# Hybrid attention step on one core: attention a step further behind the threshold search, index products spread over the heads, gate projection at a step's end, tanh gates

## What is computed

```python
scores = sum_h w_idx[h] * relu(q_idx[h] . k_idx)         # 8 index heads
_, sel = lax.top_k(where(pos_k <= pos_q, scores, -inf), 256)
att  = softmax(q . k[sel] / 8) @ v[sel]                   # 8 query heads, 2 K/V heads
conv = b_conv * conv3(c_conv * u)
mo   = softmax(q_mem . mk / 8) @ mv                       # 4 heads, 256 memory tokens
o = concat[att * silu(g_att), conv * silu(g_conv), mo * silu(g_mem)] @ w_out
y = x + rms_norm(o, g_post)
```

## Time and profile before

| | us |
|---|---|
| median of 3 runs | 2611.46 (2609.06 to 2613.33) |
| profiled execution, its own time | 2617.17 |
| span of the profiled execution | 2615.4 |
| stage A, to about | 690 |
| first output projection starts | 774.4 |
| last output projection starts | 2334.3 |
| TensorE busy, with the modelled ends of matmuls | 2233.5 |
| VectorE busy | 1492.2 |
| ScalarE busy | 1161.4 |
| mean granted TensorE clock | 0.85 |

### The profile page before, as it was taken

One profiled execution on the slowest core, in us unless ns is written; L12 is line 12 of the kernel. 1 busy time (PEld: TensorE's weight loads), 2 busy tenths in 40 slices (PEclk: granted clock), 3 DMA queues, 4 the chain that ended last, 5 costly groups with the idle time before them and its releaser, 6 DMA issues.

```text
span 2615.4 us, 34415 instructions
## 1 busy us (share of the span) xinstructions
PE 2233.5 (85%) x12592; PEld 1762.7 (67%) x12592; DVE 1492.2 (57%) x3449; ACT 1161.4 (44%) x2297; POOL 135.5 (5%) x174
## 2 busy tenths in 40 slices
PE   7999999999478888888988878888878888988765
PEld 4777777776466666676676666666666767768652
DVE  2444444443145666776787777878777842434580
ACT  1111111011025566665776766767577668432000
POOL 0000000000000000000000000000000010100004
PEclk9999999999567788777898989888889889987556
DMA  7111111111511110111011010101010010114001
GB/s 264 66 72 50 70 65 71 47 66 40 180 49 59 53 57 20 50 57 45 17 57 32 28 50 11 49 11 49 11 33 27 17 43 9 43 65 138 1 3 31
DMA packets 58411, 137.57 MB, mean 53 GB/s; under 512 B 13904, under 2 KB 26872, under 8 KB 57248
## 3 DMA queue, kind: packets, MB, share of 16 engines
q1 hardware_dynamic: 56096, 125.26, 14.3%
q0 software_dynamic: 2176, 10.49, 1.2%
HBM read 96.83 MB, written 38.90 MB: 52 GB/s over the span
## 4 chain that ended last, share of the span: by engine, by line
PE 62%; DVE 15%; ACT 13%; issue 6%; DMA 2%; SPq 1%; POOL 1%; PEld 1%; DVEq 0%; ACTq 0%; POOLq 0%; PEldq 0%
PE psum L566 12%; PE psum L599 9%; PE psum L1220 8%; PE psum L1189 7%; PE psum L1231 6%; PE psum L1212 5%; ACT sb_lowj L851 4%; PE psum L1178 3%; PE psum L1202 3%; DVE sb_junk L968 3%; ACT sb_ptb L838 2%; DVE sb_sc L953 2%; ACT sb_p L909 1%; PE psum L613 1%; DVE sb_p L987 1%
## 5 line engine op out<-in xcount | busy, mean ns | idle before, releaser
L1220 PE MATMUL psum<-sb_v,sb_ptb 128*128 128x64 f32 x2176 | 329.9, 300 | 31.0 <-ACT sb_ptb L838 30.6
L1220 PEld LDWEIGHTS psum<-sb_v,sb_ptb 128*128 128x128 f32 x2176 | 315.2, 221 | 49.4 <-ACT sb_ptb L838 48.9
L566 PE MATMUL psum<-sb_w,sb_xt 128*128 128x512 f32 (+5 forms) x1088 | 324.8, 459 | 0.5 <-DVE sb_xt L382 0.5
L851 ACT ACTIVATE sb_lowj<-sb_sc,sb_ncand,sb_scl 128x384 bf16<-128x384 f32 (+13 forms) x224 | 312.5, 1395 | 2.4
L968 DVE TENSOR_SCALAR_CACHE_REDUCE sb_junk<-sb_sc,sb_c 128x384 bf16<-128x384 f32 (+13 forms) x210 | 310.1, 1477 | 3.6
L1212 PE MATMUL psum<-sb_con,sb_p 128*128 128x128 f32 x1280 | 243.6, 320 | 52.6 <-ACT sb_p L909 31.3
L838 ACT ACTIVATE sb_ptb<-psum 128x512 f32<-128x512 f32 (+3 forms) x352 | 187.2, 533 | 185.0 <-PE psum L1212 183.8
L566 PEld LDWEIGHTS psum<-sb_w,sb_xt 128*128 128x128 f32 (+1 forms) x1088 | 178.5, 185 | 134.5 <-issue 125.1
L1231 PE MATMUL psum<-sb_wo,sb_mix 128*128 128x512 f32 x512 | 257.2, 666 | 13.5 <-DVEq L1146 13.5
L1189 PEld LDWEIGHTS psum<-sb_qa,sb_w 128*128 128x128 f32 x2048 | 250.7, 196 | 12.8 <-issue 4.8
L1189 PE MATMUL psum<-sb_qa,sb_w 128*128 128x128 f32 x2048 | 253.0, 280 | 1.3
(11 more groups left out here) (340 smaller groups left out, 2491.4 us busy)
## 6 DMA issues: line engine op xcount, KB each, us to landing
qt_s<-sb_qt SPq DMA_DIRECT2D x32, 512.0 KB, 2.8
sb_x<-in_x_prompt SPq DMA_DIRECT2D x16, 512.0 KB, 3.7
xt_s<-sb_xt SPq DMA_DIRECT2D x16, 512.0 KB, 2.6
sb_qa<-xt_s SPq DMA_DIRECT2D x16, 512.0 KB, 3.3
sb_qa<-qt_s SPq DMA_DIRECT2D x16, 512.0 KB, 3.5
sb_qa<-qt_s SPq DMA_DIRECT2D x32, 256.0 KB, 4.7
sb_xres<-in_x_prompt SPq DMA_DIRECT2D x16, 512.0 KB, 5.1
out_y_prompt<-sb_y SPq DMA_DIRECT2D x16, 512.0 KB, 3.0
```

Of the source, the lines that this page charges most:

```text
L566: mm = pe.matmul(out, m.xt[:, p, k, 0:n], m.w1[:, k, lo:hi], start=(k == 0), stop=(k == KD - 1))
L851: ins = act.activation(m.lowj[:, 0:w], m.sc[u % 3][:, 0:w], ACT.Sign, bias=m.ncand[:, p], scale=m.scl[:, p], accum_out=m.tally[:])
L1220: mm = pe.matmul(o, m.ptb[:, g, x * P:(x + 1) * P], v, start=st, stop=sp)
```

## The change

STEPS gets one more value, and step i now attends tile j = i-3, so a mask made at the end of step i-1 is read one step later; `m.bias` has three buffers instead of two and `m.gate` two. `pairs_at` gives the index pairs of a step: an eighth of them before the head loop, an eighth behind each of the heads 0 to 6, each pair behind a group's turn and values. `scores_of` is one head ahead for all widths. ScalarE takes 33 of the 47 refinement operations within the heads, 2 behind the gates and 12 behind the memory exponentials; VectorE takes 8 searches within the heads, 2 before and 1 after the attention output's scaling, and 4 behind the memory maximum; a search no longer has other work between its operations. The gate projection of tile j+1, its gating and its memory scores stand at the end of step j, ahead of the output projection of tile j. `select(i-1)` comes before `hand_over(i)`. Gates are (1 + tanh(z/2)) z on every path, with the factor of a half moved into the norm and `g_post`; the two table loads of each step are gone. The load of the second index queries is issued ahead of most weights. The diff, cut to its core:

```diff
         cv = m.cv[:].rearrange("p b n -> p (b n)")
         ch.inc(dve.tensor_tensor(cv, m.pc[1][:, 0:256], cv, ALU.mult))
-        ch.link(dve.tensor_scalar(m.eg[:], m.eg[:], 1.0, None, ALU.add))
-        ch.link(dve.reciprocal(m.eg[:], m.eg[:]))
-        dve.tensor_tensor(m.eg[:], m.pc[1][:, 256:512], m.eg[:], ALU.mult).then_inc(s.zc_read, 1)
+        dve.scalar_tensor_tensor(out=m.eg[:], in0=m.eg[:], scalar=1.0, in1=m.pc[1][:, 256:512], op0=ALU.add,
+                                 op1=ALU.mult).then_inc(s.zc_read, 1)
         dve.wait_ge(s.zc_read, 2 * i + 2)
         if not isinstance(i, int) or i >= 1:
             dve.wait_ge(s.st_cm, 16 * i)
...
@@ -668,11 +665,13 @@
 
 
 
-STEPS = range(1, NT + 2)
+STEPS = range(1, NT + 3)
 BITS = 31
 LOW = 16
 HIGH = BITS - LOW
 LOW_OPS = 3 * LOW - 1
+LOW_TAIL = 14
+HIGH_TAIL = 7
...
+def heads_at(h):
+
+    return [h + 1] if h + 1 < NH else []
+
+
+def pairs_at(i, h):
+
+    if not indexed(i + 1):
+        return []
+    pairs = [(c, hp) for c in chunks(width(i + 1), 512) for hp in range(4)]
+    if not attended(i - 3):
+        return pairs if h < 0 else []
+    n = len(pairs)
+    return pairs[n * (h + 1) // NH:n * (h + 2) // NH] if h < NH - 1 else []
...
+        if k == 0:
+            load_idx(TOPK // P + 1)
...
-        act.activation(m.gate[:, 0:512], m.turn[z[0][0]][:], ACT.Exp, scale=-1.0).then_inc(s.zact, 1)
...
+        act.activation(gate[:, 0:512], m.turn[z[0][0]][:], ACT.Tanh, scale=0.5).then_inc(s.zact, 1)
...
-        act.wait_ge(s.zact, 3 * j + 3)
-        act.activation(m.gate[:], m.gate[:], ACT.Ln, bias=m.ones[:]).then_inc(s.zln, 1)
-        act.wait_ge(s.zln, 2 * j + 1)
-        act.activation(m.gate[:], m.gate[:], ACT.Exp, scale=-1.0).then_inc(s.zln, 1)
+        act.activation(gate[:, 512:768], m.turn[z[1][0]][:, 256:512], ACT.Tanh, scale=0.5).then_inc(s.zact, 1)
...
-            q = refine(u, q)
-            for n, c in enumerate(chunks(w, 512)):
-                take_group(("t", j, h, c))
-                if n < 2:
-                    q = refine(u, q)
...
+            for h in range(NH):
+                pairs = pairs_at(i, h)
+                act.wait_ge(s.nb, NH * j + h + 1)
+                act.activation(m.p[:, h % 2, 0:w], m.p[:, h % 2, 0:w], ACT.Exp, bias=m.nmax[:, h:h + 1], scale=SCALE,
+                               accum_out=m.l[:, h:h + 1]).then_inc(s.exp, 1)
+                end = share(LOW_OPS - LOW_TAIL, NH, h)
+                for n, c in enumerate(chunks(w, 512)):
+                    take_group(("t", j, h, c))
+                    if n < len(pairs):
+                        rectify(i, *pairs[n])
+                    refine(u, q, min(2, end))
+                    q, end = q + min(2, end), end - min(2, end)
+                for pair in pairs[len(chunks(w, 512)):]:
+                    rectify(i, *pair)
+                refine(u, q, end)
+                q += end
+        if attended(j + 1):
+            gates(j + 1)
+            refine(u, q, 2)
+            q += 2
+            memory(j + 1)
+        refine(u, q, LOW_OPS - q)
+        if attended(j):
+            act.wait_ge(s.y_done, j + 1)
...
+            for h in range(NH):
+                mask(j, h)
+                if h == 0:
+                    if j >= 1:
+                        normalise(j - 1)
+                    if indexed(i):
+                        begin(i)
+                its = share(HIGH - HIGH_TAIL, NH, h) if indexed(i) else 0
+                for c, hp in pairs_at(i, h - 1):
+                    for e in range(2):
+                        accumulate(i + 1, c, 2 * hp + e)
+                    if its:
+                        search(i, done)
+                        done, its = done + 1, its - 1
+                for _ in range(its):
+                    search(i, done)
+                    done += 1
...
+            if indexed(i):
+                for _ in range(2):
+                    search(i, done)
+                    done += 1
+            dve.wait_ge(s.exp, NH * (j + 1))
+            ch.link(dve.reciprocal(m.l[:], m.l[:]))
...
+            if indexed(i):
                 search(i, done)
                 done += 1
...
+        if attended(j + 1):
+            gate(j + 1)
...
+            dve.sem_inc(s.gated, 1)
+        if attended(j + 1):
+            memory_max(j + 1)
...
-            assert done == HIGH
+            for it in range(done, HIGH):
+                search(i, it)
+        if i - 1 < NT:
+            select(i - 1)
+        if indexed(i):
             hand_over(i)
-        if indexed(i - 1):
-            select(i - 1)
...
+            for h in range(NH):
...
+                for x in heads_at(h):
+                    scores_of(j, x)
+                pe.wait_ge(s.exp, NH * j + h + 1)
+                pairs = pairs_at(i, h)
+                for n, c in enumerate(chunks(width(j), 512)):
+                    turn_group(("t", j, h, c), m.p[:, h % 2, :], c[0], c[1] // P)
+                    next_values()
+                    waiting.append((h, c))
+                    if n < len(pairs):
+                        index_pair(i + 1, *pairs[n])
+                for pair in pairs[len(chunks(width(j), 512)):]:
+                    index_pair(i + 1, *pair)
+            while waiting:
+                next_values()
+        if attended(j + 1):
+            pe.wait_ge(s.xt2_ld, 16 * (j + 2))
+            for b in range(8):
+                gate_block(j + 1, b)
+        if attended(j):
+            pe.wait_ge(s.att, j + 1)
+            turn_group(("ta", j), m.att, 0, 4)
+        if attended(j + 1):
+            memory_scores(j + 1)
+        if attended(j):
+            pe.wait_ge(s.cm_ld, 16 * (j + 1))
+            if j == 0:
+                pe.wait_ge(s.wo_ld, 32)
+            pe.wait_ge(s.gated, j + 1)
+            project_out(1, (4, 5, 6, 7, 0, 1, 2, 3), 4, 3)
+            project_out(0, (4, 5, 6, 7, 0, 1, 2, 3), 4, 3).then_inc(s.y_done, 1)
```

489 lines of the change are left out of this document (210 added, 279 removed).

## The result

| | before | after |
|---|---|---|
| median, us | 2610.26 (4 runs) | 2951.18 (2945.82 to 2956.86, 4 runs) |
| ratio to before | | 1.131, 95% interval 1.128 to 1.133 |
| span of the profiled execution | 2615.4 | 2943.7 |
| first output projection starts | 774.4 | 810.4 |
| eleven steps, j=1 to 11 | 1081.4 | 1372.5 |

What follows compares the result with a forecast made beforehand. A step was taken as a chain across in-order engines, none of them full. Start +42, eleven steps +163 and last four -43 gave +162 on 2617.2, so 2779, less 5.7 for the median: 2773 us, range 2565 to 2860.

Steps and rivals of the forecast that it cites:

- First output projection at about 816: Start of the kernel: first output projection at about 816 us instead of 774.4, +42, with 790 to 825 possible.
- The six periods of 5.3: Start, between first mask and first output projection: six head periods of 5.3 us, then the gate projection of tile 1.
- A step's start: Output projection's start to second exponential: refinement, select, hand-over, then first mask; 27.9, 39.2 and 54.5 us for j=2, 6, 11.
- The head periods: Head loop, paced by ScalarE: six periods take 37.8, 50.4 and 64.2 us for j=2, 6, 11.
- The clock: Rival, chance 0.13: TensorE at half clock in head loops costs 45 to 90 us in the six lower steps; 2850.
- The link from exponential to copy: Inside each head: without refinement between them, ScalarE idles 0.74 us from the exponential's end to its first group's copy.
- The last head to its values: Step's end, after the six head periods: 3.3, 5.6 and 7.6 us for j=2, 6, 11.
- Gate projection exposed, 14.8: Step's end: the gate projection takes 14.8 us, with little work for VectorE and none for ScalarE until the first half.
- The eleven steps: Steps j=1 to 11, interpolated from 87.4, 113.6 and 144.7 us: 1245 against 1081, +163.
- The last four steps: Steps j=12 to 15: together 436 us against 478.5, -43.
- VectorE sets the pace, 2556: Rival, chance 0.16: ScalarE's idle links are absorbed, so VectorE's work sets each step; eleven steps -54, median 2556.
- Even, 2611: Rival, chance 0.06: in middle steps head-loop growth equals what leaves the index phase; only start and end count, 2611.

Runs made afterwards that it cites:

- e8: Changed kernel with LOW_TAIL 2 and HIGH_TAIL 3, moving all but two refinement operations and three searches into the heads: 2953.45 us.
- e2: Changed kernel with four unread 512-column TensorE passes ahead of each head's wait for its exponential: 2883.88 us, 1.106 of the kernel before.
- e1: Changed kernel with values one group behind the turns instead of two: 2896.38 us, 1.111 of the kernel before.
- e5: Changed kernel with values one group behind the turns and four unread passes ahead of each exponential's wait: 2860.99 us, 1.097 of the kernel before.
- e7: Changed kernel with ScalarE's head order as exponential, refinement, copy, refinement, rectifier: 2804.62 us, 1.074 of the kernel before.
- e9: Changed kernel with values one group behind, filler passes, gate projection behind the output projection, and refinement first: 2641.49 us, 1.015 of the kernel before.
- e12: Kernel before with tanh gates, second index queries loaded early, and two unread passes ahead of exponential waits in steps j=0 to 7: 2575.59 us, ratio 0.988.
- e6: Changed kernel with all index pairs of a step ahead of its head loop instead of spread over heads: 3009.11 us, 1.153 of the kernel before.
- e10: Changed kernel with refinement first, select behind the masks of heads 0 and 1, at most one index pair ahead of the loop: 2799.53 us, ratio 1.074.

## Why the prediction was right or wrong

The step that failed is the head loop. It was summed at TensorE's full clock and with values one group behind the turns; the clock granted over the eleven steps was 0.77, and values stood two groups behind. With that the heads took more than their terms. Of the 178 us between forecast and median, 128 lie in the eleven steps and 45 in the last four; the start took 6 off, and 11 come from the step from the profiled execution to the median, 5 up where 6 down was taken. Item by item:

- **First output projection at about 816.** It was 810.4, close in part by luck: the first mask came at 745.3 and not at 756, with the weights in earlier, and from there to the output projection it took 65.1 for 60. The six periods of 5.3 are right. The two waits of TensorE for queries in that stretch of the changed kernel are 7.8 and 6.6 us:

```profile
PE psum L1237 <- DMA sb_qa<-qt_s: 7.8, 1, 7.8
PE psum L1201 <- DMA sb_qi<-qt_s: 6.6, 1, 6.6
```

- **A step's start.** Right. The second exponential was put at 27.9, 39.2 and 54.5 for j=2, 6 and 11 and came at 28.3, 38.9 and 55.0; first masks at 18.8, 24.1 and 30.7 against 19.1, 24.5 and 31.1. That this chain is ScalarE's refinement, select, hand-over, first mask holds; with fewer refinements and searches in it (e8) the first mask of j=6 came at 14.9.
- **The head periods: the larger part of the failure.** "The full clock is assumed throughout, as a bound from below", and that bound was then used as the likeliest value. Measured 44.5, 54.4 and 70.2 for 37.8, 50.4 and 64.2, and e2 shows that at a higher clock nearly the sum's own values come out. The clock stood as a rival with 0.13, at 2850 (its own terms, the middle of 45 to 90 on top of 2773, give 2841), and it was priced for the six lower steps alone; the granted clock was 0.77 over all eleven. It should have been in the sum: 0.64 and 0.83 in the earlier trace rows, for a TensorE with fewer waits than the sum gave it, said so.
- **The link from exponential to copy.** "The copy is next, so the 0.74 is idle" was wrong as a link: it is 1.65 or 2.87, since the copy waits for values two groups back. At full clock the total was right all the same, 1.65 + 0.32 against 0.74 + 1.33, because the same values had been counted ahead of the rectifier. At half clock it is 2.87 + 1.16: 2.06 more a head.
- **The last head to its values.** 3.3, 5.6 and 7.6 in the forecast, 5.4, 8.7 and 12.7 measured. With values one group behind (e1) it takes 4.1, 6.8 and 11.0, and with the filler too (e5) 4.1, 7.0 and 8.6. That the lag is two groups was in the code, and was not read.
- **Gate projection exposed, 14.8.** From its first product to its last it took 16.0 to 17.7 in the eleven steps, because its first half runs in part at half clock (8.5 to 10.2 us for the first 64 products, 7.4 for the other 64); in the steps of j=13 and 14, at full clock, it took 14.9. VectorE's idle time ahead of the gating product was over 10 us, as said: 15.0 for j=6.
- **The eleven steps** were +291 for +163. By place, with the forecast's own interpolation from j=2, 6 and 11, the 128 missing are: six head periods 60, last head to its values 36, from there to the output projection 15 (the gate projection above all), the step's start 2, and 15 from steps that are longer than the straight lines between the three (3 to 5 with 8 of it, 7 to 10 with 6). By cause, filler and lag together took back 92 (e5).
- **The last four steps** were +2 for -43. At j=12 the start was right (45.6 for 46.2) and the head periods were too short: 9.3 was measured for 7.8, which is 9 of the 14 us missing there, and the last head took 12.1 for 8, 4 more. Values one group behind gave back 15 of the 45 (e1) and refinement first 10 (e7), both no more than one trace may vary. The cause of the rest was not settled.
- **VectorE sets the pace, 2556.** Not seen: changing ScalarE's order alone was worth 147 us (e7). **Even, 2611.** Not seen either.

As to why the change is slower at all: e9 takes 304 to 310 of its 341 us back by three orders and a filler, one of which undoes the move of the gate projection, without undoing the spread, the extra step or tanh. So most of the loss is that ScalarE's in-order stream waits for TensorE twice in every head with nothing in between, that values stand one group too far behind, that the gate projection runs with two engines idle, and that TensorE, waiting in turn, falls to half clock. Not all is found: e12 has tanh, the early queries and a filler as well, on the same chip, and is 66 us faster than e9. By the traces e9 loses 76 us to it in the eleven steps and gains 24 in the last four. What remains of the change there (spread, extra step, the searches' and refinements' places) was not taken apart; that the spread pays is shown in the changed kernel alone (e6), and the extra step was tried in no run by itself. What the extra step was to bring was not used: select still stood ahead of the first mask, and where it was moved (e10) rectifiers waited for the sums behind it.

## What to carry to other kernels

When work is spread into a loop of links between in-order engines, write down for each engine what stands between what it hands over and what it waits for next; here refinement moved ahead of the copy and the rectifier in every head was worth 147 us of 2951. Read the lag of a software pipeline from its first entries: two groups in a list at the start stay two groups to the end. A forecast for TensorE with waits in it should price those stretches at the clock that similar stretches show, and keep full clock as the bound only.

## What the runs showed that was not expected

Unread passes made the kernel faster: 504 instructions of 166 us busy time in TensorE's waits took 67 us off (e2), since the granted clock of the loops rose from 0.50 to 0.82 at j=1; in the kernel before the same trick was worth 11 us (e12). And taking two table loads, a logarithm and an exponential out of every step of the kernel before gave 12 us in all: rows at tile 6 show 0.7 a step, because there a chain on two other engines was almost as long.
